# Moving the split activations in SBUF, and a reordered stage boundary, in a 15-stage fp32 kernel on one core

## The chip, the cores and the metric

One Trainium2 chip, one of its cores. The metric is the device time of one launch in microseconds, the median of several runs. Five engines matter: TensorE (PE; its weight loads are shown as PEld), VectorE (DVE), ScalarE (ACT), GpSimd (POOL), and SyncE (SP), which issues most transfers.

## What is computed

Three transformer-like blocks run one after the other on one sequence of 256 tokens and 1024 channels, all in fp32. Each block is a chain of stages of the form "normalise, mix or feed forward, add to x":

```python
x = x + conv_glu_ffn(rmsnorm(x, ff_norm[layer]), ff_w_up[layer], ff_conv_w[layer],
                     ff_conv_b[layer], ff_w_down[layer])                 # ffn0, ffn1, ffn6 in this form
x = x + FFN_RES * g1[:, None, :] * swiglu(h, ffn_w13[i, 0], ffn_w2[i, 0])  # ffn2 to ffn5
m = pool_ssd_mixer(h, ...)   # or mla_mixer, rwkv7 and gating, dilated attention, GLA and MoBA
x = x + g2[:, None, :] * m
return rmsnorm_2(x, final_norm_g)                                         # fin1, fin2, fin3
```

The `mod` vectors (scale, shift and gate `g`) of the second block are a product of a 1024 vector with `mod_w`.

## The kernel before

**Data.** `x` and every activation are held channel-major: 128 partitions, 8 tiles `k` of 256 tokens. A product in fp32 accuracy is made of three matmuls (`product`, lines 263 to 267): both operands are split into a high half of type fp32r and a low rest, `w_hi`, `w_lo` and `a_hi`, `a_lo`, and the terms `w_hi*a_hi`, `w_hi*a_lo` and `w_lo*a_hi` are added in PSUM. The weight tile is the operand that is loaded, the activation streams through with 256 columns. The exception is `a_unit_by_token` (lines 297 to 309), where the activation is loaded and the weight streams.

**Activations.** `h_hi` and `h_lo` hold the split result of each norm; `g_hi` and `g_lo` the split hidden layer of a feed-forward stage; `e_hi` and `e_lo` four more tiles that only the end of stage `ssd` uses. By the sizes in which they are declared (lines 159 to 187), a partition's bytes are laid out so: the weight slots `ring`, `w_hi`, `w_lo` from 0 to 73,728, `x` to 81,920, `h_hi` and `h_lo` to 98,304, `hf` and small tiles to 115,844, then the region `mix` (86,016 bytes) of the mixers. `g_hi`, `g_lo`, `zs`, `acc`, `sil`, `gf` share the start of that region, and `e_hi` and `e_lo` its end (193,668 to 201,860).

**Weights.** They come in units of 1 MB (16 tiles of 128 by 128), 335 numbered units in order of use, through three slots. For unit `n` SP loads `ring`, ScalarE makes `w_hi` (`hi`, lines 248 to 254) once the slot's old unit is done on TensorE, VectorE makes `w_lo` (`lo`, lines 256 to 261; on GpSimd for the down units of `ffn2` to `ffn6`), and TensorE takes 48 matmuls over it. A-units (`a_unit`) produce two blocks of 128 channels, B-units (`b_unit`) add two input tiles into all eight output blocks, banks 2 to 5.

**A feed-forward stage** (`ffn_order`, line 542) has 22 up units (A) and 11 down units (B): two ups, then ten times two ups and a down, then the last down; turns of "up, up, down" run in a loop. Each up's result passes ScalarE, VectorE (`gf`), ScalarE (`g_hi`) and then `g_lo`, which GpSimd makes, or VectorE in `ffn0` and `ffn1` (`dve_alone`). In `ffn0` to `ffn3` VectorE also computes the `mod` vectors (`mod_dve`, line 520), two per turn.

**The boundary between stages.** Each engine has its own queue in program order and waits on semaphores. In the last B-unit TensorE goes by pairs of blocks and signals each pair. VectorE adds each pair into `x` (`residual_dve`, line 414), ScalarE squares it into `hf` (line 346), and TensorE sums the squares over the channels with 16 one-column fp32 matmuls (line 375), of which the trace shows two records each. Then ScalarE takes the root, VectorE the reciprocal, TensorE spreads it over the partitions (line 383, two matmuls), VectorE scales `x` into `hf` (line 399), ScalarE makes `h_hi` tile by tile (lines 358, 359), VectorE `h_lo` (lines 406, 409). The first unit of the next stage (`a_unit` with `parts`, lines 275 to 289) starts as the first tile of `h_hi` is there: all high-half terms of block 0, then of block 1, then the `h_lo` terms. After `fin1` and `fin2` a second norm follows directly.

**Order of the `lo` steps there.** The next stage's first three units are prepared around the boundary. After the last up unit VectorE makes `lo` of the first; the second is made at the last but one down unit (by GpSimd in `ffn2` to `ffn6`); the third, `owed`, behind the next stage's norm. In a mixer's last stage VectorE makes `lo` of the units before the residuals.

## Time and profile before

| | us |
|---|---|
| three runs | 2505.61, 2498.98, 2504.65 |
| median | 2504.65 |
| the profiled execution: its time | 2504.1 |
| its span, first to last instruction | 2502.2 |
| TensorE busy in the span | 2350.2 |
| VectorE, ScalarE, GpSimd busy | 1454.8, 1163.0, 452.2 |

TensorE's busy time is modelled, since matmuls overlap: a matmul of 256 columns is shown 0.28 us long and the next starts 0.11 to 0.12 us after it. So the distance between starts, not the length, tells the rate. "Granted clock" is the share of TensorE's full speed: 1.00 is 2.4 GHz, 0.50 is 1.2 GHz.

### The profile page before, as it was taken

Reading aid. Unit: us, or ns where it says so; the run is one execution under the profiler, and the core shown is the slowest. Engines: PE = TensorE matmul, PEld = TensorE weight load, DVE = VectorE, ACT = ScalarE, POOL = GpSimd, SP = SyncE. Lnnn points to the kernel's source line nnn. Section 1 sums busy time; section 2 is a strip of 40 time slices with the busy share of each in tenths; the row PEclk is TensorE's granted clock in tenths of the full one; section 3 lists DMA queues with packets and bytes.
Section 4 is the critical chain, followed back from the end, with each engine's and each line's share of the span. In section 5 each row is a group of like instructions: output and inputs, shape, how many; then the busy total and the mean of one; then the engine's idle time right before and its main releaser. Section 6 shows DMA issues by size and latency. Waiting matters only on the chain.

```text
span 2502.2 us, 46392 instructions
## 1 busy us (share of the span) xinstructions
PE 2350.2 (94%) x18464; PEld 2270.4 (91%) x18464; DVE 1454.8 (58%) x2006; ACT 1163.0 (46%) x1543; POOL 452.2 (18%) x203
## 2 busy tenths in 40 slices
PE   8989999998999899998899999999999999889998
PEld 7879799997999799996899999997899999778998
DVE  4553389945699669875469943355533344345544
ACT  5411265545555444464344444445544444454654
POOL 0022000000000045320035424410044300000442
PEclk9868799999999799996899989988999999888999
DMA  6200168742488368652268745543354545523552
GB/s 238 102 1 1 60 252 304 283 155 85 165 306 309 145 252 348 239 186 79 94 231 326 282 152 184 178 150 116 115 186 174 180 144 181 168 76 104 186 182 100
DMA packets 62214, 438.92 MB, mean 175 GB/s; under 512 B 7228, under 2 KB 7612, under 8 KB 9638
## 3 DMA queue, kind: packets, MB, share of 16 engines
q1 hardware_dynamic: 59472, 430.75, 47.0%
q0 software_dynamic: 976, 2.63, 0.7%
q10 hardware_dynamic: 1670, 4.17, 0.5%
q8 instruction: 72, 1.18, 0.2%
q14 instruction: 24, 0.20, 0.0%
HBM read 434.89 MB, written 2.62 MB: 175 GB/s over the span
## 4 chain that ended last, share of the span: by engine, by line
PE 84%; DVE 6%; ACT 4%; issue 4%; DMA 1%; DVEq 0%; SPq 0%; ACTq 0%; POOLq 0%; POOL 0%
PE ps L265 20%; PE ps L267 20%; PE ps L266 20%; PE ps L375 3%; PE ps L280 2%; PE ps L282 2%; PE ps L288 2%; DVE mix L524 1%; ACT w_hi L254 1%; DMA ring<-in_weights 1%; PE ps L1314 1%; PE ps L889 1%; PE ps L975 1%; PE ps L383 1%; PE ps L976 1%
## 5 line engine op out<-in xcount | busy, mean ns | idle before, releaser
L265 PE MATMUL ps<-h_hi,w_hi 128*128 128x256 f32 x3512 | 998.2, 284 | 6.5 <-DVE h_lo L2116 4.5
L267 PE MATMUL ps<-h_hi,w_lo 128*128 128x256 f32 x3512 | 996.3, 284 | 0.0
L266 PE MATMUL ps<-h_lo,w_hi 128*128 128x256 f32 x3512 | 996.1, 284 | 0.0
L260 DVE TENSOR_TENSOR w_lo<-ring,w_hi 128x2048 fp32r<-128x2048 f32 x286 | 656.4, 2296 | 582.7 <-ACT w_hi L254 579.0
L254 ACT ACTIVATE w_hi<-ring 128x2048 fp32r<-128x2048 f32 x335 | 639.8, 1911 | 192.7 <-PE ps L267 182.3
L265 PEld LDWEIGHTS ps<-h_hi,w_hi 128*128 128x128 f32 x3512 | 676.6, 193 | 8.6 <-DVE h_lo L2116 4.8
L266 PEld LDWEIGHTS ps<-h_lo,w_hi 128*128 128x128 f32 x3512 | 676.4, 193 | 0.1
L267 PEld LDWEIGHTS ps<-h_hi,w_lo 128*128 128x128 f32 x3512 | 676.4, 193 | 0.0
L669 POOL TENSOR_TENSOR g_lo<-gf,g_hi 128x256 f32 (+1 forms) x110 | 167.4, 1522 | 1507.2 <-ACT g_hi L603 1507.2
L265 PE MATMUL ps<-g_hi,w_hi 128*128 (+1 forms) x1232 | 343.1, 278 | 14.5 <-DVE g_lo L652 13.9
L266 PE MATMUL ps<-g_lo,w_hi 128*128 (+1 forms) x1232 | 342.1, 278 | 0.0
L267 PE MATMUL ps<-g_hi,w_lo 128*128 (+1 forms) x1232 | 341.9, 278 | 0.0
L260 POOL TENSOR_TENSOR w_lo<-ring,w_hi 128x2048 fp32r<-128x2048 f32 x49 | 233.2, 4760 | 77.9 <-ACT w_hi L254 77.7
L265 PEld LDWEIGHTS ps<-g_hi,w_hi 128*128 128x128 f32 x1232 | 233.4, 189 | 15.1 <-DVE g_lo L652 14.3
L266 PEld LDWEIGHTS ps<-g_lo,w_hi 128*128 128x128 f32 x1232 | 233.3, 189 | 0.0
L267 PEld LDWEIGHTS ps<-g_hi,w_lo 128*128 128x128 f32 x1232 | 232.9, 189 | 0.0
L524 DVE CUSTOM_DVE_ANT_0 mix<-mix 128x1024 f32<-128x1024 f32 x144 | 215.1, 1530 | 9.9 <-DMA mix<-in_modw 9.9
L603 ACT ACTIVATE g_hi<-gf 128x256 f32 (+1 forms) x154 | 64.1, 416 | 244.3 <-DVE gf L644 244.3
L280 PE MATMUL ps<-h_hi,w_hi 128*128 128x256 f32 x360 | 110.5, 333 | 15.8 <-ACT h_hi L358 8.6
L598 ACT ACTIVATE sil<-ps 128x256 f32<-128x256 f32 x88 | 33.6, 382 | 168.9 <-PE ps L267 159.6
L626 DVE SCALAR_TENSOR_TENSOR acc<-zs,vec,acc 128x255 f32<-128x255 f32 x132 | 57.8, 480 | 92.9 <-ACT acc L589 92.7
L282 PE MATMUL ps<-h_hi,w_lo 128*128 128x256 f32 x360 | 107.6, 326 | 0.0
(387 smaller groups left out, 2554.7 us busy)
## 6 DMA issues: line engine op xcount, KB each, us to landing
ring<-in_weights SPq DMA_DIRECT2D x335, 1024.0 KB, 4.8
mix<-in_modw SPq DMA_DIRECT2D x72, 1024.0 KB, 4.9
mix<-in_c_ssd ACTq DMA_DIRECT2D x1, 1536.0 KB, 6.2
bias_rows<-mix POOLq DMA_DIRECT2D x1, 1536.0 KB, 36.2
x<-in_x SPq DMA_DIRECT2D x1, 1024.0 KB, 4.9
mix<-in_c SPq DMA_DIRECT2D x2, 512.0 KB, 4.4
mix<-bias_rows POOLq DMA_DIRECT2D x1, 1024.0 KB, 8.2
out_xT<-hf SPq DMA_DIRECT2D x1, 1024.0 KB, 4.3
```

The source lines that it names most:

```text
L254: act.activation(w_hi[:, n % SLOTS], ring[:, n % SLOTS], ACT.Copy).then_inc(hi_ready, 1)
L260: dve.tensor_tensor(w_lo[:, n % SLOTS], ring[:, n % SLOTS], w_hi[:, n % SLOTS], ALU.subtract).then_inc(lo_ready[n % SLOTS], 1)
L265: pe.matmul(o, w[0], a_hi, start=first, stop=False, **kw)
L266: pe.matmul(o, w[0], a_lo, start=False, stop=False, **kw)
L267: return pe.matmul(o, w[1], a_hi, start=False, stop=last, **kw)
L280: pe.matmul(o, w_hi[:, s, c:c + P], h_hi[:, k], start=b == 0 and k == 0, stop=False, skip_group_check=True)
L282: pe.matmul(o, w_lo[:, s, c:c + P], h_hi[:, k], start=False, stop=False, skip_group_check=True)
L375: done = pe.matmul(ps[sums][:, c:c + 1], hf[:, dst + k, c * P:(c + 1) * P], ones[:, 0:1], start=k == 0 and c == 0, stop=k == kb - 1 and c ...
L524: done = dve.tensor_tensor_reduce(out=m_ring[:, j, b], in0=m_ring[:, j, b], in1=m_cs, scale=1.0, scalar=0.0, op0=ALU.mult, op1=ALU.add, ac ...
L603: act.activation(dst, gf[:, e], ACT.Copy).then_inc(ghi_done, 1)
L626: dve.scalar_tensor_tensor(out=acc[:, e, half, 1:T], in0=zs[:, e, half, 0:T - 1], scalar=vat("fcw" + name[3:], 44 + 22 * half + m + i * 2) ...
L669: pool.tensor_tensor(dst, gf[:, m % 2], src, ALU.subtract).then_inc(glo_done, 1)
```

## The change

Six edits.

1. `h_hi` and `h_lo` are declared behind `mix`. A pad of 3,072 bytes is put ahead of the region, and inside it `zs`, `acc`, `sil`, `gf` come first and `g_hi`, `g_lo` behind them. By the declared sizes `h_hi` and `h_lo` then lie at 188,548 to 204,932, `g_hi` starts at 114,820 (before: 115,844), `mix` at 102,532, `e_hi` at 180,356.
2. Sum of squares: the last two blocks are handled one by one; GpSimd adds squares (0+1, 2+3, then both, and 4+5), and TensorE sums four tiles instead of eight, into bank 0.
3. `keep_warm`: matmuls of a constant with a constant into bank 1, whose results nobody reads: one behind the first tile of sums, one behind the sums, two behind the spreading matmuls.
4. In a feed-forward stage's last unit block 7 goes to bank 6, and block 6 is signalled by itself.
5. The first unit of a stage goes tile by tile through both blocks.
6. `lo` steps: the one that VectorE made ahead of the residuals is cut into two halves, one between the first and second residual, one behind the last; the second unit's `lo` after every feed-forward stage goes to GpSimd, behind its additions of the next norm.

```diff
-        h_hi = sb("h_hi", [P, KD, T], F32R)
-        h_lo = sb("h_lo", [P, KD, T], F32R)
...
+        sb("below_mix", [P, 768])
         with ExitStack() as over:
-            g_hi = over.enter_context(nc.sbuf_tensor("g_hi", [P, KF, T], F32R))
-            g_lo = over.enter_context(nc.sbuf_tensor("g_lo", [P, KF, T], F32R))
             zs = over.enter_context(nc.sbuf_tensor("zs", [P, 2, 2, T], F32))
             acc = over.enter_context(nc.sbuf_tensor("acc", [P, 2, 2, T], F32))
             sil = over.enter_context(nc.sbuf_tensor("sil", [P, 2, T], F32))
             gf = over.enter_context(nc.sbuf_tensor("gf", [P, 2, T], F32))
+            g_hi = over.enter_context(nc.sbuf_tensor("g_hi", [P, KF, T], F32R))
+            g_lo = over.enter_context(nc.sbuf_tensor("g_lo", [P, KF, T], F32R))
         with ExitStack() as over:
             over.enter_context(nc.sbuf_tensor("below", [P, mixed_size - 8 * T], F32))
             e_hi = over.enter_context(nc.sbuf_tensor("e_hi", [P, 4, T], F32R))
             e_lo = over.enter_context(nc.sbuf_tensor("e_lo", [P, 4, T], F32R))
         mix = sb("mix", [P, mixed_size])
+        h_hi = sb("h_hi", [P, KD, T], F32R)
+        h_lo = sb("h_lo", [P, KD, T], F32R)
...
+        def lo_half(dve, n, half):
+
+            cols = slice(half * UNIT // 2, (half + 1) * UNIT // 2)
+            if half == 0:
+                dve.wait_ge(hi_ready, n + 1)
+            done = dve.tensor_tensor(w_lo[:, n % SLOTS, cols], ring[:, n % SLOTS, cols], w_hi[:, n % SLOTS, cols],
+                                     ALU.subtract)
+            if half == 1:
+                done.then_inc(lo_ready[n % SLOTS], 1)
+
...
             if parts:
-                for b in range(2):
-                    for k in range(ks):
+                for k in range(ks):
+                    pe.wait_ge(*after(f"act:{parts}.hi{k}"))
+                    for b in range(2):
                         c, o = (2 * k + b) * P, ps[bank][:, b * T:(b + 1) * T]
-                        if b == 0:
-                            pe.wait_ge(*after(f"act:{parts}.hi{k}"))
                         pe.matmul(o, w_hi[:, s, c:c + P], h_hi[:, k], start=b == 0 and k == 0, stop=False,
                                   skip_group_check=True)
                         pe.matmul(o, w_lo[:, s, c:c + P], h_hi[:, k], start=False, stop=False, skip_group_check=True)
-                for b in range(2):
-                    for k in range(ks):
+                for k in range(ks):
+                    if k % 2 == 0:
+                        pe.wait_ge(*after(f"dve:{parts}.lo{k // 2}"))
+                    for b in range(2):
                         c, o = (2 * k + b) * P, ps[bank][:, b * T:(b + 1) * T]
-                        if b == 0 and k % 2 == 0:
-                            pe.wait_ge(*after(f"dve:{parts}.lo{k // 2}"))
                         done = pe.matmul(o, w_hi[:, s, c:c + P], h_lo[:, k], start=False, stop=b == 1 and k == ks - 1,
                                          skip_group_check=True)
...
-        def b_unit(pe, n, i, a_hi, a_lo, first, last, tag=None):
+        def down_block(b, far):
+
+            return ps[6][:, 0:T] if far and b == 7 else ps[2 + b // 2][:, (b % 2) * T:(b % 2 + 1) * T]
+
+        def b_unit(pe, n, i, a_hi, a_lo, first, last, tag=None, far=False):
 
             pe.wait_ge(lo_ready[n % SLOTS], n // SLOTS + 1 + i)
             s = n % SLOTS
 
             tiles = [(kk, b) for kk in range(2) for b in range(8)]
             if tag:
-                tiles = [(kk, b) for q in range(4) for kk in range(2) for b in (2 * q, 2 * q + 1)]
+                tiles = [(kk, b) for q in range(3) for kk in range(2) for b in (2 * q, 2 * q + 1)]
+                tiles += [(0, 6), (1, 6), (0, 7), (1, 7)]
             for kk, b in tiles:
                 c = (8 * kk + b) * P
 
-                done = product(pe, ps[2 + b // 2][:, (b % 2) * T:(b % 2 + 1) * T],
-                               (w_hi[:, s, c:c + P], w_lo[:, s, c:c + P]), a_hi(kk), a_lo(kk),
-                               first and kk == 0 and b % 2 == 0, last and kk == 1 and b % 2 == 1,
+                done = product(pe, down_block(b, far), (w_hi[:, s, c:c + P], w_lo[:, s, c:c + P]), a_hi(kk), a_lo(kk),
+                               first and kk == 0 and (b % 2 == 0 or far and b == 7), last and kk == 1 and b % 2 == 1,
                                skip_group_check=True)
-                if tag and kk == 1 and b in (1, 3, 5):
+                if tag and kk == 1 and b in ((1, 3, 5, 6) if far else (1, 3, 5)):
                     done.then_inc(*step(f"pe:{tag}.b{b // 2}"))
...
+        def square_tiles(tag, kb):
+
+            return [(0, 2), (2, 2), (4, 2), (6, 1), (7, 1)] if tag in STAGES else [(k, 2) for k in range(0, kb, 2)]
...
-            for q in range(kb // 2):
+            for q, (k, n) in enumerate(square_tiles(tag, kb)):
                 for w in ready(q):
                     act.wait_ge(*w)
-                act.activation(hf[:, dst + 2 * q:dst + 2 * q + 2], src[:, 2 * q:2 * q + 2],
-                               ACT.Square).then_inc(*step(f"act:{tag}.sq{q}"))
+                act.activation(hf[:, dst + k:dst + k + n], src[:, k:k + n], ACT.Square).then_inc(*step(f"act:{tag}.sq{q}"))
...
         def norm_banks(tag):
-            return (3, 5) if tag == "mla.kv" else (6, 7)
+            return (3, 5) if tag == "mla.kv" else (0, 7) if tag in STAGES else (6, 7)
+
+        def norm_pool(pool, tag):
+
+            for q, (a, b) in enumerate(((0, 1), (2, 3), (0, 2), (4, 5))):
+                if q == 2:
+                    pool.wait_ge(*after(f"pool:{tag}.pair1"))
+                else:
+                    pool.wait_ge(*after(f"act:{tag}.sq{b // 2}"))
+                pool.tensor_tensor(hf[:, a], hf[:, a], hf[:, b], ALU.add).then_inc(*step(f"pool:{tag}.pair{q}"))
+
+        def keep_warm(pe, n):
+
+            for _ in range(n):
+                pe.matmul(ps[1][:, 0:T], ones, tri, start=True, stop=True)
 
         def norm_pe(pe, tag, kb, dst=0):
-            norm_pe_sums(pe, tag, kb, dst)
+            if tag not in STAGES:
+                norm_pe_sums(pe, tag, kb, dst)
+                norm_pe_over(pe, tag)
+                return
+            sums = ps[norm_banks(tag)[0]]
+            for k, w in ((0, "pool:{}.pair2"), (4, "pool:{}.pair3"), (6, "act:{}.sq3"), (7, "act:{}.sq4")):
+                pe.wait_ge(*after(w.format(tag)))
+                for c in range(NCH):
+                    done = pe.matmul(sums[:, c:c + 1], hf[:, k, c * P:(c + 1) * P], ones[:, 0:1],
+                                     start=k == 0 and c == 0, stop=k == 7 and c == 1, skip_group_check=True)
+                if k == 0:
+                    keep_warm(pe, 1)
+            done.then_inc(*step(f"pe:{tag}.ss"))
+            keep_warm(pe, 1)
             norm_pe_over(pe, tag)
+            keep_warm(pe, 2)
...
+        def residual_dve(dve, tag, last_unit, factor=None, between=None):
+            for q, (k, n) in enumerate(square_tiles(tag, KD)):
+                if q == 1 and between is not None:
+                    lo_half(dve, between, 0)
+                far = tag.startswith("ffn")
+                dve.wait_ge(*(after(f"pe:{tag}.b{q}") if q < 3 + far else (unit_done, last_unit + 1)))
+                for b in range(k, k + n):
+                    o = down_block(b, far)
+                    if factor is None and n == 1:
+                        done = dve.tensor_tensor(x[:, b], o, x[:, b], ALU.add)
+                    elif factor is not None:
+                        done = dve.scalar_tensor_tensor(out=x[:, b], in0=o, scalar=factor(b), in1=x[:, b],
                                                         op0=ALU.mult, op1=ALU.add)
+                if factor is None and n == 2:
+                    done = dve.tensor_tensor(x[:, k:k + 2], ps[2 + q][:].rearrange("p (a b) -> p a b", a=2),
+                                             x[:, k:k + 2], ALU.add)
                 done.then_inc(*step(f"dve:{tag}.res{q}"))
+            if between is not None:
+                lo_half(dve, between, 1)
...
+        def between_of(s):
+
+            n = last_unit[s] + (1 if s.startswith("ffn") else 2)
+            return n if n < UNITS else None
...
-            turns = FFN_TURNS - (name == order[-1])
+            turns = FFN_TURNS - 1
...
@@ -642,17 +699,19 @@
                     dve.wait_ge(taps_done, k + 4 + i * 8)
                 val = acc[:, e, 1] if conv else ps[e][:, T:2 * T]
                 dve.tensor_tensor(gf[:, e], val, sil[:, e], ALU.mult).then_inc(g_done, 1)
-                if m % 2 == 1:
+                if m % 2 == 1 and m < KF - 1:
                     lo(dve, n + SLOTS, i)
                 if name in MODS and not isinstance(i, int):
                     mod_dve(dve, MODS[name], m - 4, i)
+                elif name in MODS and m >= KF - 2:
+                    mod_dve(dve, MODS[name], m - KF + 2, FFN_TURNS - 1)
                 if name in dve_alone:
...
             def down(j, n, i):
-                if name in dve_alone and j < 10:
+                if name in dve_alone and j < 9:
                     lo(dve, n + SLOTS, i)
...
+        def ffn_pool_owed(pool, n):
+
+            if n < UNITS:
+                pool.wait_ge(lo_ready[(n - 1) % SLOTS], (n - 1) // SLOTS + 1)
+                lo(pool, n)
...
-                        residual_dve(dve, s, last_unit[s], norm_of[s][2])
+                        residual_dve(dve, s, last_unit[s], norm_of[s][2], between_of(s))
 
             @block.gpsimd
             def _(pool):
                 pool.wait_ge(const_in, 16)
+                owed = None
                 for s in STAGES:
+                    norm_pool(pool, s)
+                    if owed and not s.startswith("fin"):
+                        ffn_pool_owed(pool, owed)
+                        owed = None
+                    if s.startswith("ffn"):
+                        owed = last_unit[s] + 2
                     if s.startswith("ffn") and s not in dve_alone:
```

The other mixers get the same `owed=2`; waits on `res3` become waits on `res4`; the squares of a stage behind `fin1` or `fin2` wait for tiles 1, 3, 5, 6, 7. In the remaining part of `norm_pe`, norms inside `mla` go by the old functions.

How the queues change, at the boundary behind `ffn3` (names: `ps2` to `ps7` are PSUM banks; `x4` is a count). On VectorE, from the last of the `mod` step on, before:

```order
L539 TENSOR_SCALAR modr<-mod 128x8
L422 SCALAR_TENSOR_TENSOR x<-ps2,modr,x 128x256 x2
L422 SCALAR_TENSOR_TENSOR x<-ps3,modr,x 128x256 x2
L422 SCALAR_TENSOR_TENSOR x<-ps4,modr,x 128x256 x2
L422 SCALAR_TENSOR_TENSOR x<-ps5,modr,x 128x256 x2
L393 RECIPROCAL rtok<-root 128x2
L399 SCALAR_TENSOR_TENSOR hf<-x,modg,ps7 128x256 x8
L409 SCALAR_TENSOR_TENSOR h_lo<-hf,mod,h_hi 128x256 x8
```

and now (lines of the changed kernel):

```order
L596 TENSOR_SCALAR modr<-mod 128x8
L470 SCALAR_TENSOR_TENSOR x<-ps2,modr,x 128x256 x2
L269 TENSOR_TENSOR w_lo<-ring,w_hi 128x1024
L470 SCALAR_TENSOR_TENSOR x<-ps3,modr,x 128x256 x2
L470 SCALAR_TENSOR_TENSOR x<-ps4,modr,x 128x256 x2
L470 SCALAR_TENSOR_TENSOR x<-ps5,modr,x 128x256
L470 SCALAR_TENSOR_TENSOR x<-ps6,modr,x 128x256
L269 TENSOR_TENSOR w_lo<-ring,w_hi 128x1024
L438 RECIPROCAL rtok<-root 128x2
L444 SCALAR_TENSOR_TENSOR hf<-x,modg,ps7 128x256 x8
L454 SCALAR_TENSOR_TENSOR h_lo<-hf,mod,h_hi 128x256 x8
```

A half `lo` stands behind the first residual, another behind the last one, and the last pair of blocks is two rows from banks 5 and 6.

On TensorE at the same place, from the last down matmuls on, before:

```order
L267 MATMUL ps5<-g_hi,w_lo 128x256
L375 MATMUL ps6<-const,hf 128x1 x16
L383 MATMUL ps7<-const,rtok 128x128 x2
L280 MATMUL ps0<-h_hi,w_hi 128x256
L282 MATMUL ps0<-h_hi,w_lo 128x256
```

and now:

```order
L278 MATMUL ps6<-g_hi,w_lo 128x256
L276 MATMUL ps6<-g_hi,w_hi 128x256
L277 MATMUL ps6<-g_lo,w_hi 128x256
L278 MATMUL ps6<-g_hi,w_lo 128x256
L405 MATMUL ps0<-const,hf 128x1 x2
L394 MATMUL ps1<-const 128x256
L405 MATMUL ps0<-const,hf 128x1 x6
L394 MATMUL ps1<-const 128x256
L428 MATMUL ps7<-const,rtok 128x128 x2
L394 MATMUL ps1<-const 128x256 x2
L290 MATMUL ps0<-h_hi,w_hi 128x256
L292 MATMUL ps0<-h_hi,w_lo 128x256
```

Sixteen one-column matmuls became eight, four constant matmuls stand between them and the next unit, and the last block is in bank 6.

On GpSimd, from the `lo` of a down unit at the end of `ffn3`'s loop into `ffn4`, before:

```order
L260 TENSOR_TENSOR w_lo<-ring,w_hi 128x2048
L551 REGISTER_ALU
L551 COMPARE_AND_BRANCH
L669 TENSOR_TENSOR g_lo<-gf,g_hi 128x256 x4
L260 TENSOR_TENSOR w_lo<-ring,w_hi 128x2048
```

and now:

```order
L261 TENSOR_TENSOR w_lo<-ring,w_hi 128x2048
L608 REGISTER_ALU
L608 COMPARE_AND_BRANCH
L728 TENSOR_TENSOR g_lo<-gf,g_hi 128x256 x2
L389 TENSOR_TENSOR hf<-hf 128x256 x4
L261 TENSOR_TENSOR w_lo<-ring,w_hi 128x2048
L728 TENSOR_TENSOR g_lo<-gf,g_hi 128x256 x4
L261 TENSOR_TENSOR w_lo<-ring,w_hi 128x2048
```

Before, the loop's last turn held the `lo` and the rows behind it belong to `ffn4`; now the last two `g_lo` of `ffn3` stand alone, four additions of squares follow, and only then the `lo`, ahead of the four `g_lo` of `ffn4`.

## Rows read from the trace of the kernel before

**Rows 1.** The page, part 1 (totals) and the clock of part 2.
```profile
PE 2350.2 (94%) x18464; PEld 2270.4 (91%) x18464; DVE 1454.8 (58%) x2006; ACT 1163.0 (46%) x1543; POOL 452.2 (18%) x203
...
PEclk9868799999999799996899989988999999888999
```

**Rows 2.** The page, part 4: chain that ended last, by engine and line.
```profile
PE 84%; DVE 6%; ACT 4%; issue 4%; DMA 1%; DVEq 0%; SPq 0%; ACTq 0%; POOLq 0%; POOL 0%
```

**Rows 3.** Groups of TensorE by form: count, busy us, mean ns, idle before.
```profile
L265 PE MATMUL ps<-h_hi,w_hi 128*128 128x256 f32 x3512 | 998.2, 284 | 6.5 <-DVE h_lo L2116 4.5 <-DVE h_lo L2095 2.0
...
L265 PE MATMUL ps<-g_hi,w_hi 128*128 x992 | 274.5, 277 | 0.0
...
L280 PE MATMUL ps<-h_hi,w_hi 128*128 128x256 f32 x360 | 110.5, 333 | 15.8 <-ACT h_hi L358 8.6 <-ACT h_hi L359 7.2
...
L306 PE MATMUL ps<-w_hi,h_hi 128*128 128x256 f32 x160 | 46.2, 289 | 0.0
```

**Rows 4.** Timeline, TensorE: start us, length us, line; then line L266 in `od_out`.
```profile
1083.01 0.28 PE L265 MATMUL ps<-h_hi,w_hi 128*128 128x256 f32 x1
...
1089.13 0.28 PE L265 MATMUL ps<-h_hi,w_hi 128*128 128x256 f32 x1
...
1230.27 0.29 PE L265 MATMUL ps<-e_hi,w_hi 128*128 128x256 f32 x1
...
1241.06 0.28 PE L267 MATMUL ps<-e_hi,w_lo 128*128 128x256 f32 x1
...
L266 PE MATMUL ps<-h_lo,w_hi x64: 282/283/283, 616.1 to 638.7; 128*128 128x256 f32 x64
```

**Rows 5.** Windows of one turn: us, busy PE, PEld, DVE, ACT, POOL, clock, DMA share, GB/s.
```profile
424.30:441.30 17.00, 17.00 (x147) 17.00 (x146) 16.07 (x25) 10.00 (x13) 0.00 (x0) 1.00 0.81 308
741.00:758.10 17.10, 17.10 (x147) 17.10 (x146) 16.00 (x25) 10.00 (x13) 0.00 (x0) 1.00 0.80 305
...
995.00:1012.00 17.00, 17.00 (x147) 17.00 (x146) 15.41 (x14) 7.13 (x7) 7.71 (x3) 1.00 0.84 310
```

**Rows 6.** Timeline at the ends of `ffn0` and `ffn1`: first matmul of the last down unit.
```profile
497.87 0.58 PE L265 MATMUL ps<-g_hi,w_hi 128*128 128x256 f32 x1 [5.56 <-DVE g_lo L652]
...
838.65 0.58 PE L265 MATMUL ps<-g_hi,w_hi 128*128 128x256 f32 x1 [8.35 <-DVE g_lo L652]
```

**Rows 7.** Timeline at the end of `ffn3`, whose last down matmul starts at 1436.73.
```profile
1433.57 4.58 POOL L260 TENSOR_TENSOR w_lo<-ring,w_hi 128x2048 fp32r<-128x2048 f32 x1 [2.35 <-ACT w_hi L254]
...
1433.72 4.44 DVE L529 TENSOR_TENSOR mod<-m_sum,vec 128x4 f32 x1 [0.26 <-DVE m_sum L524]
...
1438.96 3.23 DVE L422 SCALAR_TENSOR_TENSOR x<-ps,modr,x 128x256 f32<-128x256 f32 x8
...
1440.55 6.99 PE L375 MATMUL ps<-const,hf 128*128 128x1 f32 x32 [3.55 <-ACT hf L346]
...
1448.09 1.22 PE L383 MATMUL ps<-const,rtok 128*128 128x128 f32 x4 [0.55 <-DVE rtok L393]
...
1450.52 0.55 PE L280 MATMUL ps<-h_hi,w_hi 128*128 128x256 f32 x1 [1.21 <-ACT h_hi L359]
```

**Rows 8.** Timeline: sums after `ffn4`; residuals after `mla`; `g_lo` behind a VectorE subtraction.
```profile
1638.61 4.21 PE L375 MATMUL ps<-const,hf 128*128 128x1 f32 x32
...
1788.15 3.22 DVE L422 SCALAR_TENSOR_TENSOR x<-ps,modr,x 128x256 f32<-128x256 f32 x8
...
1428.33 2.29 DVE L260 TENSOR_TENSOR w_lo<-ring,w_hi 128x2048 fp32r<-128x2048 f32 x1
...
1429.10 2.12 POOL L669 TENSOR_TENSOR g_lo<-gf,g_hi 128x256 f32 x1 [2.18 <-ACT g_hi L603]
```

**Rows 9.** Windows behind that boundary (columns of Rows 5); a 256-column constant matmul (line L770).
```profile
1450.50:1453.70 3.20, 3.18 (x15) 3.20 (x16) 3.20 (x10) 3.20 (x8) 0.00 (x0) 0.50 0.00 0
1453.70:1457.00 3.30, 3.30 (x29) 3.30 (x29) 3.30 (x7) 2.56 (x2) 0.00 (x0) 0.99 0.03 5
...
L770 PE MATMUL ps<-mix,const x8: 377/379/379, 38.0 to 39.5; 128*128 128x256 f32 x8
```

30 lines of the change are left out of this document (10 added, 20 removed).

## The prediction

> **What bounds the kernel now.** I read the totals, the chain of waits, TensorE's groups, and then single stretches of the timeline. TensorE is busy 2350.2 of 2502.2 us [rows 1] and carries 84% of the chain that ended last [rows 2]: two things count, the rate at which matmuls start and the time in which TensorE does no useful ones.
>
> The rate has three values. At full clock matmuls that stream `h_hi` or `h_lo` start every 120.0 ns: 51 of them between 1083.01 and 1089.13. Those that stream `e_hi` or `e_lo` start every 113.6 ns: 95 steps from 1230.27 to 1241.06 [rows 4]. That is the same code (`b_unit`), weight slots and shape as `od_out` runs with `h`, where 189 steps take 22.6 us, again 120 ns [rows 4]. So neither the shape of the unit nor its order makes the 6.4 ns, and the place of the activation is what is left. `g_hi`, in a third place above `h`, is shown at 277 ns against 284 [rows 3]. At half clock the distance is some 213 ns: 15 matmuls in 3.20 us against 29 in the next 3.30 [rows 9].
>
> The second thing is the boundary. Behind `ffn3` the last down matmul starts at 1436.73 and the next stage's first at 1450.52: 13.8 us, of which TensorE waits 3.55 for the first squares, spends 6.99 on 32 records of sums, and waits 1.21 at the end [rows 7]. Behind `ffn4` the sums follow at once and take 4.21 [rows 8]. From the timeline of all boundaries: the sums end 3.5 to 5.4 us after the last down or output matmul, mean 4.1, but 9.9 and 10.5 behind `ffn2` and `ffn3`; the clock falls 2 to 4 us after it and returns 3.1 to 5.9 us after the next stage's start (one of them in [rows 9]).
>
> Inside `ffn0` and `ffn1` VectorE is the one that is full: 16.07 us busy in a turn of 17.0, 16.00 in 17.1 [rows 5], never waiting for TensorE, and TensorE waits 5.56 and 8.35 us for the last `g_lo` [rows 6]. In `ffn2` it is 15.41 [rows 5].
>
> **The change, part by part.** The sum is made on the profiled execution, 2504.1 us; the median of the three runs, 2504.65, is within 0.6 of it.
>
> *Place of `h`.* The new place covers, nearly, the bytes where `e` runs at 113.6 ns now. The counts: 3 x 3512 of the lines 265 to 267, 3 x 360 of the first units (lines 280, 282, 288), 3 x 160 by token [rows 3] (the sister lines have the same counts), 12,096 in all. Some 375 run at half clock (L280 averages 333 ns between 282 and 413, so 39% of 720; about 1% of the rest), where 213 ns leave nothing to gain. Of the 11,720 left, 2 x 1056 stand in `ffn0` and `ffn1`, whose turns VectorE sets: there only the first five ups count, before its backlog starts, 2 x 240 less a few at half clock, at 6.4 ns 2.7 us. The other 9,608 at 6.4 ns are 61.5 us. I take off 4 for the mixers (4,700 of them, 30 us), where VectorE's and ScalarE's own chains follow the units and keep their length, and 2 for `ffn2` and `ffn3`: their turn shrinks from 16.96 to 16.4 us, and with 15.4 us of VectorE work plus its waits a backlog from the start is caught up more slowly. **58 us.** Bounds: 64 if nothing else shows up; 0 if the place is not the cause. By-token units, where `h` is loaded and the weights stream, run at 120 ns too, and nothing shows them elsewhere: 480 x 6.4 = 3 us, included, with 0 as the other end. The mixers' own operands move down by 13,312 bytes; their 128-column matmuls keep 112 ns wherever they lie today, so 0, within 2 either way.
>
> The Trainium skill ("TensorE: Matmul & The Clock Gate", Part 2, on LDWEIGHTS) speaks against this term: TensorE has two independent SBUF read ports, so that loading the next weights takes nothing from the running matmul. By that the place should not matter and the 58 us would be 0. The 120.0 against 113.6 ns above says otherwise.
>
> *Ends of `ffn0` and `ffn1`.* The `lo` ahead of the last `g_lo`, 2.29 us [rows 8], goes behind the first residual, and TensorE waits for that `g_lo` [rows 6]. **2 x 2.2 = 4.4 us.** TensorE's wait there still grows, since its ups get faster and VectorE's turn does not.
>
> *Ends of `ffn2` and `ffn3`.* The `mod` addition of four elements takes 4.44 us because GpSimd's 4.58 us `lo` runs beside it; the residuals start behind it, at 1438.96 [rows 7], where block pair 0 is ready 4.3 us before the end of the unit. That `lo` leaves, and so does VectorE's 2.29. The 3.55 us wait goes, and sums do not run wholly at half clock: 9.9 and 10.5 become about 4.6. **11 us.**
>
> *Other boundaries.* The last residual is 0.4 us shorter and 16 of 32 sum records go, 1.8 us at 0.112. But the chain through GpSimd is new. An uncontended `g_lo` of that shape is 0.74 us; beside a VectorE subtraction of two SBUF operands it takes 2.12 [rows 8]. In a feed-forward end the second `lo` half (1.15, half of 2.29) becomes ready while addition 2 runs, at +0.5 us, goes next, and addition 3 ends near +2.7; three tiles of sums, 12 records, then end at +4.1 at full and +5.3 at half clock, mean 4.5 against 3.75 now: a loss of 0.7, four times, 3 us. In a mixer's end the residual is later (3.22 us from 1788.15 behind a whole `lo` [rows 8]; now only half a `lo` stands there), addition 3 gets in first at +1.2, the sums end at +3.0 against 4.5: 1.4 us, five times, 7. The final norm and the first give 0.6 each. Second norms behind `fin1` and `fin2`: half the sums, but the owed `lo` (2.29) now blocks addition 3; 0. **Together 5 us**, between -15 (each addition at 2.5 us) and +15 (no contention). GpSimd's new 4.6 us `lo` runs from about +3 to +7.6, beside scalings of the residuals' form, which keep their 0.48 us beside GpSimd in the trace; of the `h_lo` subtractions, which it would block, the first comes at about +9.5.
>
> *Constant matmuls.* One is two records, at 0.215 or 0.12 us each [rows 9]: one fits the 0.55 us wait ahead of the spreading, two fit the 1.21 us behind it [rows 7]. Cost 0; 0.3 us a boundary if they overrun. Their use: at these boundaries the clock comes back only after TensorE has been steadily busy for a while, and steady work would now begin with the spreading, some 2.5 us earlier. I don't expect them to keep the clock from falling, since most of the 5 to 6 us stays idle. At half clock 44% of time is lost (213 to 120 ns), so 13 starts x 1.1 us less x 0.44 = **6 us**, between -5 (when it falls and rises is partly chance) and +23 (half clock after a start gone: 13 x 4.1 x 0.44).
>
> *Tile-by-tile first unit, bank 6, waits renamed.* With the clock down the matmuls are slower than the tiles come and there is nothing to gain; at full clock four matmuls per tile (0.48 us) just match ScalarE's 0.41. Cost 0, up to 1 us either way in all. The `lo` of the next units, and with them SP's loads into their slots, come 2 to 8 us later; three units of 5.8 us stand before their use.
>
> Sum: 58 + 4.4 + 11 + 5 + 6 = 84; 2504.1 - 84 = **2420 us**.
>
> **Rivals.**
> (a) *The next engine takes the gain.* TensorE's start distance falls but VectorE or transfers (310 GB/s already in rows 5) set `ffn2`, `ffn3` and the mixers. For it: VectorE's 15.4 us. Against: `ffn4` to `ffn6` and the input units have room. Half of the 58 is lost: 2450. Chance 0.13.
> (b) *The place is not the cause.* Something else that `e` and `g` have in common sets their rate; only boundaries and clock remain: 2504.1 - 26 = 2478. Against it stands the `e` row. Chance 0.08. The rule of the Trainium skill ("TensorE: Matmul & The Clock Gate", Part 2) is the mechanism by which this would come out.
> (c) *The constants hold the clock.* Half clock behind starts vanishes and the sums run at 0.112: 17 us more, 2403. Against: they fill less than a third of the gap. Chance 0.12.
> (d) *Slower.* GpSimd's additions wait for VectorE each time: 2.5 us for each of the last two moves the sums' end to about +7, 3 us later than now, at 17 norms 50 us. It decides only if addition 3 ends later than about +4 and the place gives nothing: 2504.1 - 26 + 50 = 2528. Chance 0.02. With the place's 58 it would be 2470.
> (e) The edits do what they say but two terms miss together: in the range's edges, 0.03.
>
> **How the numbers follow.** The forecast has 0.62. The range joins the forecast's unknowns (place 48 to 64, boundaries -10 to +10, clock -5 to +15) with (a) and (c): 2396 to 2458. Outside lie (b), (d) and part of (e). About 0.3% is what a measurement can tell here, 7.5 us. Faster by more: 0.96; within: 0.02; slower: 0.02.
>
> **What would show it.** Starts of `h` matmuls at full clock every 113.6 ns (right) or 120 (b). The odd `gf` of `ffn4` every 16.4 us instead of 16.96; of `ffn0` still 16.95 and of `ffn1` 17.1, with TensorE's wait at their ends at 8 us or more. In `ffn2` and `ffn3` a `mod` addition of 0.16 us at the last turn, residuals on time. Additions on GpSimd of 0.74 us, one of them lengthened behind `ffn` stages; if several are 2 us, (d). Granted clock after a start: half for 3 us instead of 4.1 on average, none for (c). The forecast fails if the start distance stays, or if TensorE shows new waits on `w_lo` or `g_lo` inside turns.

## The result, and the profile after

| | us |
|---|---|
| changed kernel, three runs | 2439.60, 2429.97, 2427.26 |
| changed kernel, the profiled execution | 2451.55 (span 2449.8) |
| changed kernel, median of the four | 2434.78 |
| kernel before beside it, median of four | 2505.13 |
| ratio, 95% interval | 0.974, 0.9717 to 0.9762 |

The change saves 70 us (2.6%). 2420 was forecast with a range of 2396 to 2458. The four executions spread over 24 us, those of before over 10.

The page of the changed kernel, parts 1, 2, 4 and 5, to be read against [rows 1 to 3]:

```profile
PE 2304.2 (94%) x18344; PEld 2211.7 (90%) x18344; DVE 1434.1 (59%) x2021; ACT 1164.3 (48%) x1558; POOL 511.3 (21%) x265
...
PEclk9869799999999899996899999998999999889999
...
PE 79%; DVE 8%; ACT 5%; issue 4%; POOL 2%; DMA 1%; DVEq 0%; SPq 0%; ACTq 0%; POOLq 0%
...
L276 PE MATMUL ps<-h_hi,w_hi 128*128 128x256 f32 x3512 | 988.5, 281 | 9.5 <-DVE h_lo L2181 4.9
...
L276 PE MATMUL ps<-g_hi,w_hi 128*128 (+1 forms) x1232 | 348.2, 283 | 9.8 <-DVE g_lo L711 9.4
...
L290 PE MATMUL ps<-h_hi,w_hi 128*128 128x256 f32 x360 | 92.5, 298 | 2.1 <-ACT h_hi L375 2.1
```

TensorE still carries the end (79% of the chain, 84% before), and GpSimd has come into the chain with 2%. The `h` matmuls are shown 3 ns shorter (284 to 281), where their starts were expected to come some 6 ns sooner, and `g` has gone the other way, from 278 over all 1232 to 283. The first units gained most: 333 to 298 ns and 15.8 to 2.1 us of waiting.

How much work starts in a stretch tells the rate better. The same 150 us of `ffn4` (96 `h` and 48 `g` matmuls a turn), columns as in [rows 5], for the kernel before, for the changed kernel, and for a second profile of the changed kernel (`e9_again`):

```profile
1470.00:1620.00 150.00, 150.00 (x1277) 150.00 (x1275) 48.10 (x36) 62.56 (x62) 67.09 (x27) 1.00 0.53 188
```
```profile
1440.00:1590.00 150.00, 150.00 (x1276) 150.00 (x1276) 46.54 (x36) 61.26 (x62) 68.87 (x27) 1.00 0.52 183
```
```profile
1440.00:1590.00 150.00, 150.00 (x1326) 150.00 (x1325) 47.06 (x38) 65.87 (x65) 68.50 (x28) 1.00 0.53 189
```

In the first profile of the changed kernel the move of `h` gained nothing in `ffn4`: 1276 matmuls against 1277. In the second it gained 49. (A row also counts the two or three matmuls that are in flight as its window begins.) The single starts explain it: before, `h` came every 120.0 ns and `g` every 113.6 on average, which is 16.97 us for a turn of 144. In the first profile all 144, `h` and `g` alike, come every 117.8 ns, which is 16.96; in the second all come every 113.3, 16.32.

I sorted all full-clock stretches of the first profile with steady starts by this distance: about 1311 us at 117.8 (`ffn0`, `ffn2` to `ffn6`, most of `gla`), 499 us at 113.3 (`ev`, `dil`, `ssd`, most of `ffn1`), none at 120. In the second profile `ffn4`, `gla` and the start of `ffn2` were at 113.3, and `dil`, `ffn1` and the end of `ssd`, at or mostly at 113.3 in the first, at 117.8.

The boundary behind `ffn3` (last down matmul starts at 1405.41), timeline, as [rows 7]; the first row is VectorE's `mod` addition of the last turn:

```profile
1399.62 0.16 DVE L586 TENSOR_TENSOR mod<-m_sum,vec 128x4 f32<-128x4 f32 x1
...
1401.57 0.87 DVE L470 SCALAR_TENSOR_TENSOR x<-ps,modr,x 128x256 f32<-128x256 f32 x2 [1.21 <-PE ps L278]
1402.36 1.21 DVE L269 TENSOR_TENSOR w_lo<-ring,w_hi 128x1024 fp32r<-128x1024 f32 x1
...
1403.50 2.71 DVE L470 SCALAR_TENSOR_TENSOR x<-ps,modr,x 128x256 f32<-128x256 f32 x6
...
1404.16 0.75 POOL L389 TENSOR_TENSOR hf<-hf 128x256 f32<-128x256 f32 x1 [5.67 <-ACT hf L364]
...
1405.11 3.19 POOL L389 TENSOR_TENSOR hf<-hf 128x256 f32<-128x256 f32 x3 [0.20 <-ACT hf L364]
...
1406.13 1.59 DVE L269 TENSOR_TENSOR w_lo<-ring,w_hi 128x1024 fp32r<-128x1024 f32 x1
...
1406.69 0.61 PE L405 MATMUL ps<-const,hf 128*128 128x1 f32 x4 [1.01 <-POOL hf L389]
...
1408.36 1.50 PE L405 MATMUL ps<-const,hf 128*128 128x1 f32 x12 [0.51 <-POOL hf L389]
...
1411.04 1.92 PE L394 MATMUL ps<-const 128*128 128x256 f32 x4
...
1412.45 0.71 PE L290 MATMUL ps<-h_hi,w_hi 128*128 128x256 f32 x1
```

The `mod` addition takes 0.16 us instead of 4.44, the residuals start 4.1 us ahead of the end of the last down matmul instead of 2 behind it, and the next stage starts 7.0 us after the start of the last down matmul instead of 13.8. TensorE waits twice for GpSimd (1.01 and 0.51 us), and no longer ahead of the spreading or of the first `h_hi`.

### The profile page after: what moved, and what is told of

Read it like the earlier page. It is cut to its first block, busy times and chain, and to the rows that moved or that the text cites. A ratio compares the mean times of both kernels' runs of the same rounds, so it can differ in the third digit from the quotient of the medians.

```text
span 2449.8 us, 46010 instructions
## 1 busy us (share of the span) xinstructions
PE 2304.2 (94%) x18344; PEld 2211.7 (90%) x18344; DVE 1434.1 (59%) x2021; ACT 1164.3 (48%) x1558; POOL 511.3 (21%) x265
## 4 chain that ended last, share of the span: by engine, by line
PE 79%; DVE 8%; ACT 5%; issue 4%; POOL 2%; DMA 1%; DVEq 0%; SPq 0%; ACTq 0%; POOLq 0%
PE ps L276 19%; PE ps L278 19%; PE ps L277 19%; DVE mix L581 2%; PE ps L290 2%; POOL hf L389 2%; PE ps L292 2%; PE ps L298 2%; PE ps L394 1%; ACT w_hi L255 1%; PE ps L405 1%; DVE w_lo L261 1%; PE ps L1379 1%; DMA ring<-in_weights 1%; PE ps L954 1%
## 5 line engine op out<-in xcount | busy, mean ns | idle before, releaser
L276 PE MATMUL ps<-h_hi,w_hi 128*128 128x256 f32 x3512 | 988.5, 281 | 9.5 <-DVE h_lo L2181 4.9
L277 PE MATMUL ps<-h_lo,w_hi 128*128 128x256 f32 x3512 | 985.6, 281 | 0.0
L278 PE MATMUL ps<-h_hi,w_lo 128*128 128x256 f32 x3512 | 985.4, 281 | 0.0
L261 DVE TENSOR_TENSOR w_lo<-ring,w_hi 128x2048 fp32r<-128x2048 f32 x273 | 627.5, 2299 | 549.5 <-ACT w_hi L255 543.9
L276 PEld LDWEIGHTS ps<-h_hi,w_hi 128*128 128x128 f32 x3512 | 668.0, 190 | 12.8 <-DVE h_lo L2181 5.1
L277 PEld LDWEIGHTS ps<-h_lo,w_hi 128*128 128x128 f32 x3512 | 667.8, 190 | 0.1
L278 PEld LDWEIGHTS ps<-h_hi,w_lo 128*128 128x128 f32 x3512 | 664.8, 189 | 0.0
L389 POOL TENSOR_TENSOR hf<-hf 128x256 f32<-128x256 f32 x60 | 56.3, 950 | 987.5 <-ACT hf L364 985.8
L261 POOL TENSOR_TENSOR w_lo<-ring,w_hi 128x2048 fp32r<-128x2048 f32 x51 | 241.5, 4735 | 72.5 <-ACT w_hi L255 71.1
L581 DVE CUSTOM_DVE_ANT_0 mix<-mix 128x1024 f32<-128x1024 f32 x144 | 223.8, 1590 | 10.4 <-DMA mix<-in_modw 10.3
L290 PE MATMUL ps<-h_hi,w_hi 128*128 128x256 f32 x360 | 92.5, 298 | 2.1 <-ACT h_hi L375 2.1
```

The source lines that it names most:

```text
L261: dve.tensor_tensor(w_lo[:, n % SLOTS], ring[:, n % SLOTS], w_hi[:, n % SLOTS], ALU.subtract).then_inc(lo_ready[n % SLOTS], 1)
L276: pe.matmul(o, w[0], a_hi, start=first, stop=False, **kw)
L277: pe.matmul(o, w[0], a_lo, start=False, stop=False, **kw)
L278: return pe.matmul(o, w[1], a_hi, start=False, stop=last, **kw)
L290: pe.matmul(o, w_hi[:, s, c:c + P], h_hi[:, k], start=b == 0 and k == 0, stop=False, skip_group_check=True)
L389: pool.tensor_tensor(hf[:, a], hf[:, a], hf[:, b], ALU.add).then_inc(*step(f"pool:{tag}.pair{q}"))
```

## The experiments

Each is compared with the kernel before on its own chip, where that took 2500.9 to 2502.4 us.

**Each half alone.** `e1_place_only` is the kernel before with edit 1 and nothing else.

> The kernel before with edit 1 alone: h_hi and h_lo behind mix, the pad, g behind zs, acc, sil, gf. The prediction's term for it was 58 us. (A) The prediction's theory: every matmul start at full clock at 113.6 ns, time 2505 - 58 = 2447. (B) Theory after reading the changed kernel's trace: the place ends the 120.0 ns, but a stream then runs throughout at either 113.3 or 117.8 ns, h and g alike, as set where the stream starts; g and e lose what they had where it is 117.8. In the changed kernel's trace 1311 us are at 117.8 and 499 us at 113.3, mean 116.5; the 14,354 full-clock matmuls of before at 116.5 instead of 120.0 and 113.6 take 28 us less: 2477, between 2467 and 2487. (C) The place does nothing by itself: 2505.

Measured: 2454.9 us (2449.9 to 2469.6), ratio 0.9819, interval 0.9779 to 0.986: 46.8 us, between (A) and (B). Two windows of its profile, in `ffn3` and in `ffn4`:

```profile
1250.00:1400.00 150.00, 150.00 (x1326) 150.00 (x1325) 129.50 (x109) 64.59 (x65) 75.14 (x27) 1.00 0.76 306
```
```profile
1440.00:1590.00 150.00, 150.00 (x1276) 150.00 (x1276) 48.58 (x38) 63.85 (x66) 66.32 (x27) 1.00 0.52 187
```

`ffn3`, at 117.8 in both profiles of the changed kernel, is at 113.3 here, and `ffn4` at 117.8. In this profile about 1414 us were at 113.3 and 333 at 117.8, and none at 120: the place does end the 120 ns. My 28 us under (B) failed because it took the first profile's mixture of rates for a fixed one.

`e2_rest_only` is the other half; `g_hi` and `g_lo` also go back ahead of `zs`:

```diff
         x = sb("x", [P, KD, T])
+        h_hi = sb("h_hi", [P, KD, T], F32R)
+        h_lo = sb("h_lo", [P, KD, T], F32R)
...
-        sb("below_mix", [P, 768])
```

> The changed kernel with edit 1 undone (h_hi and h_lo back behind x, no pad, g ahead of zs): only the boundary edits 2 to 6. The prediction gave them 26 us: 2479. If the place is worth only 28 of the 70 us measured, these are worth about 42: 2463, because less of the time is at half clock (272 us of steady matmuls against 337). h should start every 120.0 ns and g every 113.6 ns again, the gf turn of ffn4 be 16.96 us.

Measured: 2469.4 us (2468.8 to 2472.9), ratio 0.9868, interval 0.9852 to 0.9885: 32.3 us. The rates are those of before again: 1275 matmuls in 150 us of `ffn4`. With the fixed rates the spread is gone too, 4 us instead of 24. The parts alone sum to 79 us, where the whole gave 70.

**Is the rate a state, and what changes it?** `e3_steer_low` and `e4_steer_high` differ in one operand (each has one of the two lines):

```diff
+            for _ in range(2 if steer else 0):
+                pe.matmul(ps[7][:, 0:256], w_hi[:, s, 0:P], w_hi[:, s, 0:T], start=True, stop=True)   # e3
+                pe.matmul(ps[7][:, 0:256], w_hi[:, s, 0:P], h_hi[:, 0], start=True, stop=True)        # e4
             for b in range(0 if parts else blocks):
```

> The changed kernel with two more matmuls of 256 columns ahead of the second and each further pair of up units, 70 times, whose moving operand is w_hi (in the lower part of SBUF, as h was before), into bank 7, which nobody reads. In the trace of before, g ran at 113.6 ns right behind h at 120.0 ns, every time. (S) If the rate of a stream is a state that is kept until something disturbs it, and a moving operand from the low place always puts it into the 113.3 ns state, ffn2 to ffn6 run at 113.3 throughout: some 900 us at 117.8 become 866, less 50 x 0.24 = 12 us for the added matmuls (ffn0 and ffn1 hide theirs): 2435 - 34 + 12 = 2413. (T) If 117.8 belongs to something else (traffic, addresses of g), the distances stay and the time is 2435 + 12 = 2447.

> The control of the kernel with w_hi as the added moving operand: the same two matmuls, 70 times, but their moving operand is h_hi, in the high place. (S) A state that only the low place resets: distances stay as they were at the stream's start, 2435 + 12 = 2447, other stretches possibly at the other rate. If any added matmul resets it, the result is that of the other kernel. (T) 2447.

Times: 2445.9 us, where (S) had 2413, and 2447.2, as expected. The profiles tell more. Three turns of `ffn3` in a row with the low operand, then the same three with the high one:

```profile
1242.00:1252.00 10.00, 10.00 (x91) 10.00 (x90) 2.63 (x2) 4.41 (x7) 4.98 (x2) 1.00 0.51 197
1259.00:1269.00 10.00, 10.00 (x87) 10.00 (x87) 9.21 (x7) 2.79 (x3) 6.61 (x2) 1.00 0.60 223
1275.00:1285.00 10.00, 10.00 (x90) 10.00 (x90) 9.22 (x7) 3.31 (x3) 6.80 (x2) 1.00 0.66 261
```
```profile
1242.00:1252.00 10.00, 10.00 (x91) 10.00 (x90) 2.63 (x2) 4.43 (x7) 4.85 (x2) 1.00 0.54 205
1259.00:1269.00 10.00, 10.00 (x91) 10.00 (x90) 9.21 (x7) 2.88 (x3) 6.68 (x2) 1.00 0.64 226
1275.00:1285.00 10.00, 10.00 (x91) 10.00 (x90) 9.22 (x7) 3.46 (x3) 6.84 (x2) 1.00 0.67 265
```

With the low operand the rate turns over at each pair: 91, 87, 90. It does so at all 70 pairs, 113.3 to 117.8 or back. With the high one it never changes at a pair. That settles (S): the rate is a state that the stream keeps, and added matmuls with both operands in the low place (`w_hi` is their loaded operand too) change it. What I had wrong is that two of them would always lead to 113.3: they turn it over.

> The changed kernel with N more matmuls of w_hi (low place) as moving operand ahead of the second and each further pair of up units, N by stage: ffn0 1, ffn1 5, ffn2 1, ffn3 3, ffn4 4, ffn5 6, ffn6 8. Two of them turned the rate over each time (113.3, 117.8, 113.3, ...), two with the high place never. (S1) The state is only turned over, by the number: odd and even N differ, and 8 alternates as 2 did. (S2) A long enough row of low-place matmuls reaches the 120.0 ns rhythm and what follows is at 113.3 ns each time, as g behind 96 h in the kernel before: from some N up (I expect 6 or 8) all turns at 113.3. Time about 2435 + 70 x 4 x 0.12 - 15 = 2450, of no use by itself.

The edit is that of `e3_steer_low` with N in the place of 2. Time 2448.8 us. After 1, 3 and 5 the turns stayed as they were, 1 in a stream at 117.8 too. After 4 they alternate, here in `ffn4` (88, 90, 87):

```profile
1420.00:1430.00 10.00, 10.00 (x88) 10.00 (x86) 4.92 (x3) 3.52 (x5) 2.62 (x2) 1.00 0.48 186
1437.00:1447.00 10.00, 10.00 (x90) 10.00 (x90) 2.63 (x2) 3.25 (x4) 4.61 (x1) 1.00 0.51 185
1454.00:1464.00 10.00, 10.00 (x87) 10.00 (x86) 2.63 (x2) 3.00 (x4) 4.61 (x1) 1.00 0.49 192
```

After 6 and 8 all turns were at 113.3, but these streams were at 113.3 from the start, so whether six free a stream from 117.8 was open. (S1), by which 8 would alternate as 2 did, is out.

**Steering on purpose.** `e8_steer_once` puts six low-place matmuls ahead of the second up unit of `ffn2` to `ffn6`. `e12_steer_slow` adds two more ahead of the third, to turn the stream over.

```diff
+            for _ in range(steer):
+                pe.matmul(ps[7][:, 0:T], w_hi[:, s, 0:P], w_hi[:, s, 0:T], start=True, stop=True)
...
-                a_unit(pe, n, m % 2, i, parts=parts if m == 0 else None)
+                a_unit(pe, n, m % 2, i, parts=parts if m == 0 else None,
+                       steer={1: 6, 2: 2}.get(m, 0) if name in ("ffn2", "ffn3", "ffn4", "ffn5", "ffn6") else 0)
```

In `e8_steer_once` the table has only `1: 6`.

> The changed kernel with six matmuls of w_hi as moving operand, once in each of ffn2 to ffn6, ahead of the second up unit. In the scan, what followed six or eight such matmuls was always at 113.3 ns when they came in a 113.3 ns stream; from a 117.8 ns stream two or four led to 113.3 as well; six from 117.8 were not seen. (S) The state holds for the rest of the stage: ffn2 to ffn6 at 113.3 throughout. In the changed kernel's trace they were at 117.8 for about 925 us, which saves 35 us, less 5 x 0.7 = 3.5: 2451.6 - 31.5 = 2420 for such an execution, and 2407 to 2422 for all, with less spread than the 24 us of the changed kernel. (T) If the rate comes back to 117.8 by itself within a stage, 2435 to 2440.

> The kernel that steers once (2423.8 us), with two more of those matmuls ahead of the third up unit of ffn2 to ffn6: the six put the stream at 113.3 ns, the two should turn it over to 117.8 for the rest of the stage. This prices the state in executions that are not profiled. (S) Five stages of 185 us at 117.8 instead of 113.3, less the first two units: 5 x 173 x 0.038 = 33 us more, plus 5 x 0.24: 2458, between 2448 and 2465, which is above all but none or one of the changed kernel's nine executions (2420.8 to 2451.6). (T) If the start distance that the profile shows is not what the time depends on, 2425 as the kernel that steers to 113.3.

Measured: 2423.8 us (2418.6 to 2435.5) and 2453.9 us (2448.0 to 2460.3), ratios 0.9696 and 0.9808 with intervals that don't meet (0.9673 to 0.9719, 0.9789 to 0.9826). 150 us of `ffn4` in each:

```profile
1425.00:1575.00 150.00, 150.00 (x1326) 150.00 (x1325) 48.10 (x36) 64.32 (x65) 70.87 (x28) 1.00 0.55 194
```
```profile
1440.00:1590.00 150.00, 150.00 (x1276) 150.00 (x1275) 46.58 (x36) 61.99 (x63) 70.05 (x27) 1.00 0.51 182
```

The first lies just above the 2407 to 2422 expected. In both profiles every one of the five stages did as steered and kept it to its end or near it. The difference of 30 us (33 expected) is the price of the state, in executions that are mostly not profiled. One of the ten streams, `ffn2` in `e12_steer_slow`, was at 117.8 as the six came, and was at 113.3 behind them; the other nine were at 113.3 anyway.

> The changed kernel, unaltered, for a second profile and more times. (S) If each stage draws its rate when its stream starts, other stages than in the first profile run at 117.8, and the executions spread over 20 to 30 us around 2435 to 2440, where before spreads over 5 to 10. (T) If the rate belongs to the stage (its addresses or traffic), the same stages are at 117.8: ffn0, ffn2 to ffn6, gla.

2427.7 us (2420.8 to 2441.5), ratio 0.9695. The first profile's stages are not the second's, so (S) holds for the rate, though the time lies below its 2435 to 2440. Over both sets the changed kernel has nine executions, median 2428.7, mean 2432.4; the steered one has five, median 2423.8, mean 2424.5. The ratios, 0.9695 and 0.9696, are the same, so steering to 113.3 is not shown to beat the changed kernel: in most of its executions enough stages seem to run at 113.3 without it. The two profiled ones (2451.6 and 2441.5 us) are the slowest of their sets.

**Where the low place ends.** `e10_g_low` drops the pad and puts `g_hi` first, at byte 99,460.

```diff
-        sb("below_mix", [P, 768])
         with ExitStack() as over:
+            g_hi = over.enter_context(nc.sbuf_tensor("g_hi", [P, KF, T], F32R))
+            g_lo = over.enter_context(nc.sbuf_tensor("g_lo", [P, KF, T], F32R))
             zs = over.enter_context(nc.sbuf_tensor("zs", [P, 2, 2, T], F32))
```

> The changed kernel without the pad and with g_hi ahead of zs, acc, sil, gf: g_hi tile m begins at byte 99,460 + 1,024 m, g_lo at 121,988, h stays at 184 KB. This looks for the border between the place of 120.0 ns and the other. g products of tiles below the border should run at 120 ns, those above at 113 or 118. If it lies at 98,304 (below all of them), none does; if at 106,496, tiles 0 to 6; if at 114,688, tiles 0 to 14. Time within 2430 to 2465.

One execution, 2436.5 us. No `g` tile runs at 120: over ten starts in a row the mean is never above 118.4 ns. `h` up to byte 98,304 did run at 120 [rows 4]. So the low place ends between 98,304 and 99,460, and for the end of the 120 ns the 1 KB shift of `g` and the pad play no part.

**Which operand counts.** The by-token units swap the roles: `h` is loaded, and the weights (24,576 to 73,728) are the moving operand. 15 us of them in `dil`, in the kernel before, in the changed kernel and in `e9_again`:

```profile
560.00:575.00 15.00, 15.00 (x127) 15.00 (x127) 5.99 (x3) 6.83 (x6) 0.00 (x0) 1.00 0.55 206
```
```profile
547.00:562.00 15.00, 15.00 (x135) 15.00 (x134) 6.88 (x3) 6.46 (x5) 0.00 (x0) 1.00 0.56 206
```
```profile
547.00:562.00 15.00, 15.00 (x129) 15.00 (x129) 6.88 (x3) 5.58 (x5) 0.00 (x0) 1.00 0.51 189
```

With `h` low as well these 192 matmuls start every 120.0 ns; with `h` in the high place they start every 113.3 or 117.8, as the units ahead of them, although their moving operand is still low. So the 120 ns belong to matmuls whose two operands both lie low, and a low moving operand alone neither brings them nor turns the rate over. The added matmuls of `e3`, `e5`, `e8` and `e12` have both operands low. They also stream the very tile that they load; whether that plays a part wasn't tried.

**The small terms, on the kernel with fixed rates.** `e6_rest_no_constants` takes `keep_warm` out of `e2_rest_only`:

```diff
-                if k == 0:
-                    keep_warm(pe, 1)
             done.then_inc(*step(f"pe:{tag}.ss"))
-            keep_warm(pe, 1)
             norm_pe_over(pe, tag)
-            keep_warm(pe, 2)
```

`e7_rest_no_pairs` takes GpSimd's additions out, so that TensorE sums eight tiles:

```diff
-            for k, w in ((0, "pool:{}.pair2"), (4, "pool:{}.pair3"), (6, "act:{}.sq3"), (7, "act:{}.sq4")):
+            for k, w in ((0, "act:{}.sq0"), (1, "act:{}.sq0"), (2, "act:{}.sq1"), (3, "act:{}.sq1"),
+                         (4, "act:{}.sq2"), (5, "act:{}.sq2"), (6, "act:{}.sq3"), (7, "act:{}.sq4")):
...
-                    norm_pool(pool, s)
```

`e11_more_constants` doubles the constants:

```diff
             sums = ps[norm_banks(tag)[0]]
+            keep_warm(pe, 2)
...
             done.then_inc(*step(f"pe:{tag}.ss"))
-            keep_warm(pe, 1)
+            keep_warm(pe, 2)
             norm_pe_over(pe, tag)
-            keep_warm(pe, 2)
+            keep_warm(pe, 4)
```

> The kernel with edits 2 to 6 alone (2469.4 us), with the constant matmuls left out as well; its rates are fixed by the place (h 120.0, g 113.6), so that small terms can be measured on it. The prediction gave the constant matmuls 6 us by an earlier rise of the clock: 2475. (C) If they shorten the half-clock stretches behind the boundaries more than that (from 6.8 or 10.2 us in the trace of before to 3.4 us in most places of the new traces), 13 x 4 to 5 us x 0.44 = 23 to 28 us: 2495, and the stretches are 6.8 us and longer again. (D) No effect on the clock: 2469 or a little less.

Measured: 2479.5 us (2477.8 to 2482.6). The constants are worth 10.1 us, between (C) and the forecast's 6. The 4 us behind the start of the stage after `ffn4`, with the constants (`e2_rest_only`) and without:

```profile
1620.80:1624.80 4.00, 4.00 (x30) 3.96 (x29) 4.00 (x12) 4.00 (x8) 0.10 (x1) 0.83 0.64 219
```
```profile
1622.90:1626.90 4.00, 4.00 (x20) 4.00 (x21) 4.00 (x12) 4.00 (x8) 0.00 (x0) 0.54 0.65 248
```

The granted clock is 0.83 against 0.54, and 30 matmuls are counted against 20. Over the eleven starts behind a stage half clock lasts 1.1 us on average with the constants and 4.7 without. That alone would be 11 x 3.6 x 0.44 = 17 us; the whole span's half-clock time, though, is shorter by only 17 us (322 against 339), which at 0.44 is 7.5, since other stretches were longer in that profile.

> The kernel with edits 2 to 6 alone (2469.4 us), without GpSimd's additions of squares: TensorE sums all eight tiles (32 records), each as its square is there; the last two by single tiles, block 7 in its bank, constants and lo steps as changed. By the prediction the pairing loses 0.7 us behind four feed-forward stages and gains up to 1.4 behind mixers, with 5 us for all boundaries together: 2469 to 2476. If TensorE, being busy with sums earlier, keeps its clock up, this kernel could be faster: 2460 to 2465. The second norms behind fin1 and fin2 should lose their 2.4 us again, since no addition waits behind the owed lo.

Measured: 2469.1 us (2464.9 to 2470.3), as with the pairs (2469.4). The pairing shows no gain: TensorE's longer sums take the time that it waited for GpSimd. Behind `fin2` the next stage starts 15.6 us after the end of the last down matmul instead of 19.4, behind `fin1`, against what I expected, 19.4 instead of 17.8.

> The kernel with edits 2 to 6 alone (2469.4 us), with eight constant matmuls at a boundary instead of four: two ahead of the sums, one behind the first tile, two behind the sums (was one), four behind the spreading (was two). Leaving the four out cost 10 us. (C) If the half-clock stretches behind the boundaries (3.4 us in ten places, longer in others) now vanish, up to 13 x 3.4 x 0.44 = 19 us more: 2450. (D) If the added ones only run past the waits: at 0.24 us each and half clock 0.43, up to 0.8 us a boundary, 2480. I expect 2460 to 2466.

Measured: 2471.7 us (2469.9 to 2474.5), no gain. TensorE behind `ffn4`, whose last down matmul ends at 1617.87:

```profile
1618.96 0.61 PE L405 MATMUL ps<-const,hf 128*128 128x1 f32 x4 [0.22 <-POOL hf L388]
...
1620.62 1.50 PE L405 MATMUL ps<-const,hf 128*128 128x1 f32 x12 [0.52 <-POOL hf L388]
1621.98 1.75 PE L393 MATMUL ps<-const 128*128 128x256 f32 x4
1623.53 1.06 PE L428 MATMUL ps<-const,rtok 128*128 128x128 f32 x4
1624.38 2.56 PE L393 MATMUL ps<-const 128*128 128x256 f32 x8
1626.59 0.47 PE L289 MATMUL ps<-h_hi,w_hi 128*128 128x256 f32 x1
```

The clock still falls in the gap, at half clock the constants take twice as long, and they hold up the spreading and the first unit: the start comes at +8.7 us instead of +7.0. Behind the eleven starts half clock is all but gone, from 11.9 us in all to 0.6, which at 0.44 is worth 5 us, not the 19 of (C). The gaps, from the start of the last down or output matmul to the next stage, grow from 98.8 to 110.5 us. The rest of the span's half clock, inside the mixers, differs by some 30 us between these profiles (223 to 261 over four kernels whose mixers are the same), so what the two are worth together can't be read from the profiles; measured, no gain is left.

## Why the prediction was right or wrong

The time fell within the range, 15 us above the forecast. That it did is no evidence for one fixed rate: a kernel steered to 113.3 ns (2423.8 us) and one steered to 117.8 (2453.9) both lie in the range. Step by step:

- **What bounds the kernel**: right. The rate at which matmuls start and the boundaries, with the clock behind them, are where the time was gained.
- **Place of `h`, 58 us**: the cause was right, the size not. Alone it measured 47 us (35 to 55 by the interval). The step that failed is "9,608 at 6.4 ns": it took 113.6 ns, which `e` and `g` had, as the rate of the new place. Both had it right behind `h` at 120.0 ns. Without such a stream next to it, the new place has two rates, and the count that matters is how many matmuls run at 117.8. That is 1311 us of the first profile, but some 180 of them stand in `ffn0`, whose turn VectorE sets: it lasts 191.3 us at 117.8 there and 190.9 at 113.3 in `e8_steer_once`. The other 1130 us, some 9,600 matmuls at 4.5 ns, cost 43 us. `g`, which I left at nothing, pays part of it. 2451.6 less 43 is 2409, so the other terms together were larger than forecast. The by-token units, put in at 3 us with 0 as the other end, did leave 120 ns. The bounds, 0 to 64, did hold the value; the chosen value sat near the upper end because one row of `e` was its evidence.
- **The Trainium skill's rule** ("TensorE: Matmul & The Clock Gate", Part 2), two independent read ports, from which I worked out that the place does not matter, is not borne out here: by it `e1_place_only` would have been 2502, and it is 2455. Rival (b) is out. Why two operands in the low place cost more isn't shown.
- **Ends of `ffn0` and `ffn1`, 4.4 us**: right in sum. TensorE's waits for the last `g_lo` are 3.00 and 6.38 us (5.56 and 8.35 before), together 4.5 less. My sign of 8 us or more did not come, in part by the draw of the rate: at 117.8, as in `ffn0`, a turn of TensorE is as long as before, and where `ffn0` ran at 113.3 (`e8_steer_once`) the wait was 5.97. In `ffn1`, mostly at 113.3, TensorE also waited six times inside the turns for VectorE's `w_lo`, 1.8 us in all. The prediction had named new waits on `w_lo` inside turns as a sign of failure; they are the gain of the ups, which VectorE's turn takes back. VectorE's turns stayed 16.95 and 17.13 as said.

```profile
488.82 0.38 PE L276 MATMUL ps<-g_hi,w_hi 128*128 128x256 f32 x1 [3.00 <-DVE g_lo L711]
...
817.95 0.58 PE L276 MATMUL ps<-g_hi,w_hi 128*128 128x256 f32 x1 [6.38 <-DVE g_lo L711]
```

- **Ends of `ffn2` and `ffn3`, 11 us**: right. In `e2_rest_only` the next stage starts 4.3 and 6.4 us sooner, 10.7 together.
- **Other boundaries, 5 us**: right in sum, 5.7 in `e2_rest_only` with the second norms and the final one in it, but made of other parts. Behind `ffn3` GpSimd's last addition ends 2.6 us after the last matmul (2.7 forecast), and the sums behind `ffn2` to `ffn5` at 4.1 to 4.2; behind `ffn0` and `ffn1` they end at 2.6 and 2.5, so that `ffn0`, `ffn1`, `ffn4` and `ffn5` gain 0.4 on average instead of losing 0.7. Behind the mixers the sums end at 4.4 on average (4.5 before), not at 3.0: of the 60 additions the median is 0.74 us but the longest 2.80, and TensorE waits 34.0 us for them in all.

```profile
L389 POOL TENSOR_TENSOR hf<-hf x60: 717/736/2804, 8.6 to 2438.1; 128x256 f32<-128x256 f32 x60
```

- **Second norms, 0**: wrong by 3 us. Behind `fin2` the owed `lo` (2.28 us) holds the additions, which take 5.07 instead of 3 us, and TensorE waits 4.39 us:

```profile
1949.45 5.07 POOL L389 TENSOR_TENSOR hf<-hf 128x256 f32<-128x256 f32 x4 [4.91 <-ACT hf L364]
...
1950.98 2.28 DVE L261 TENSOR_TENSOR w_lo<-ring,w_hi 128x2048 fp32r<-128x2048 f32 x1
1953.89 1.01 PE L405 MATMUL ps<-const,hf 128*128 128x1 f32 x4 [4.39 <-POOL hf L389]
```

- **Constant matmuls, 6 us**: right in kind, low. 10 us, with half clock after a start down from 4.1 to 1.2 us where 3 was forecast. I had credited them with an earlier rise of 1.1 us. Rival (c), the clock held throughout, did not come: at ten of eleven boundaries inside the kernel it still falls.
- **Rivals**: (a) explains little. In the changed kernel `ffn4` had room and stood at 16.96 us a turn because of the state. Its mechanism does show where `ffn2` and `ffn3` run at 113.3: in `e8_steer_once` they end with waits for GpSimd's last `g_lo`, 3.3 us together, where I had taken off 2. (d) had its mechanism, additions of up to 2.80 us behind VectorE, but about one per norm and not two.

```profile
1015.16 0.38 PE L276 MATMUL ps<-g_hi,w_hi 128*128 128x256 f32 x1 [2.25 <-POOL g_lo L731]
...
1385.43 0.38 PE L276 MATMUL ps<-g_hi,w_hi 128*128 128x256 f32 x1 [1.02 <-POOL g_lo L731]
```

The profiled execution is 31 us above the forecast. The state cost it some 43 us; so the other terms gave some 11 more than forecast. `e2_rest_only` shows 6 of these (32 where 26 were forecast), of which 4 are the constants by `e6_rest_no_constants`. The remainder I can't assign.

## What to carry to other kernels

Read the start distance of matmuls for each operand and each stage, and in two executions, before a mean is multiplied by a count; a rate seen next to another stream may be borrowed from it. When one kernel's executions spread more than another's, compare two profiles of it stage by stage: here the spread was the finding. Matmuls that only keep the clock up help where TensorE would wait anyway, and here brought no more once they ran past the wait.

## What the runs showed of the hardware

- With both operands below byte 98,304 of a partition, 256-column matmuls with a weight load each start every 120.0 ns at full clock; with the moving operand above 99,460 (`h`, `g`), or the loaded one (`h` at 188,548 and up in the by-token units), every 113.3 or every 117.8 ns. No long stream had both operands high.
- Which of the two a stream has was mostly kept for as long as it ran without waits, up to 180 us. It differs between executions of one program. One start that came 15 ns late was followed by the change, at 898.57 in `e9_again`, where `ffn2` went from 113.3 to 117.8; starts behind waits and clock changes also often show the other rate.
- Two matmuls with both operands low turned it over each time, four too; after 1, 3 or 5 it was as before, and six left 113.3 in ten of ten streams, one of which came from 117.8. I know no cause for this and tested none. The weight loads are shown with it: 188 ns each in the window of `ffn4` at 113.3, and 192 for one in three at 117.8.
- A GpSimd addition with a median of 0.74 us took up to 2.80 beside VectorE's subtraction of two SBUF operands; all 14 of the 60 that took 0.98 or more overlap one. The Trainium skill ("SBUF — State Buffer", "Who interferes with whom") has the two engines share a port pair under an exclusive lock; the trace agrees.
